# Two transformer blocks on one core: softmax weights divided before their transposes, two heads' values in one pass of column tiles, a new order of the first block's slots, and six gate units moved among the mixing units

## The reference

```python
def first_block(x, ...):            # 2 layers
    h = rms_norm(x, ln1_gain[l])
    proj = h @ w_in[l]              # q, k, v, gates and latents of three mixers
    o_nsa = nsa_mixer(...)          # 6 heads: gate0*compressed + gate1*selected + gate2*window
    o_mla = mla_mixer(...)          # 5 heads, softmax attention over 96 numbers
    o_ret = retention_mixer(...)    # 5 heads, decayed scores, group norm, silu gate
    mixed = concatenate([o_nsa, o_mla, o_ret])      # 384 + 320 + 320 columns
    x = x + mixed @ w_out[l]
    x = x + square(relu(rms_norm(x) @ w_up[l])) @ w_down[l]

def masked_softmax(s, mask):
    p = exp(s - max(s)) * mask
    return p / sum(p)

def hybrid_layer(x, ...):           # second block, 2 layers
    u = h @ w_in                    # pool, conv, q, k, v, gate_logits (3 x 1024)
    y_pool, y_conv = pool_mixer(...), b_conv * causal_short_conv(...)
    y_attn = moba_attention(q, k, v)                # 8 heads of 64
    merged = gates0 * (y_pool @ p_pool) + gates1 * (y_conv @ p_conv) + gates2 * (y_attn @ p_attn)
    x = x + g1 * (merged @ w_out)
    x = x + g2 * ((silu(h2 @ w_gate) * (h2 @ w_up)) @ w_down)
```

## Time and profile before

| | before |
|---|---|
| median of three runs | 1517.23 us (1515.48 to 1518.75) |
| the profiled execution, its own time | 1515.29 us |
| span of the profiled execution | 1513.5 us |
| busy share of the span: PE | 98% |
| PE weight load | 95% |
| DVE | 72% |
| ACT | 52% |
| POOL | 4% |
| granted clock of TensorE | 1.00 throughout |
| bytes moved | 296.56 MB, 195 GB/s over the span |

### The profile page before, as it was taken

The page is one execution under the profiler, slowest core; times in us unless marked ns, Lnnn a source line. Parts: engine busy times, 40 slices in busy tenths (PEclk is TensorE's granted clock), DMA queues, the critical chain, the costliest instruction groups (busy, mean ns, idle before and its releaser), DMA issues.

```text
span 1513.5 us, 29309 instructions
## 1 busy us (share of the span) xinstructions
PE 1481.1 (98%) x12148; PEld 1441.9 (95%) x12148; DVE 1085.0 (72%) x1931; ACT 783.4 (52%) x1370; POOL 63.3 (4%) x73
## 2 busy tenths in 40 slices
PE   8999999999999999999999999999999999999999
PEld 8888999999888999999999989999999999999999
DVE  8777788887777788788884577665569646766653
ACT  6555577435555487434555545444444554454442
POOL 0000000000000000000030030000003003100000
PEclk9999999999999999999999999999999999999999
DMA  8233389886234378887444444555434434454551
GB/s 327 80 142 121 142 308 341 325 335 259 101 113 167 140 265 328 325 341 271 165 161 149 168 143 151 197 179 195 173 144 158 168 141 167 139 194 170 194 184 67
DMA packets 42435, 296.56 MB, mean 196 GB/s; under 512 B 5056, under 2 KB 5312, under 8 KB 6848
## 3 DMA queue, kind: packets, MB, share of 16 engines
q1 hardware_dynamic: 41888, 294.67, 53.5%
q10 hardware_dynamic: 416, 0.02, 0.0%
HBM read 293.62 MB, written 1.05 MB: 195 GB/s over the span
## 4 chain that ended last, share of the span: by engine, by line
PE 74%; DVE 12%; DMA 6%; ACT 4%; issue 2%; POOL 1%; SPq 0%; DVEq 0%; ACTq 0%
PE acc L771 22%; PE acc L772 21%; PE acc L773 21%; DMA ring<-stream 6%; DVE wL L1688 5%; ACT wH L1333 2%; PE ps_t L898 1%; DVE ring L1678 1%; PE ps_s L885 1%; PE ps_o L908 1%; PE ps_o L907 1%; PE ps_s L883 1%; PE acc L972 1%; PE acc L867 1%; POOL region L2419 1%
## 5 line engine op out<-in xcount | busy, mean ns | idle before, releaser
L1688 DVE TENSOR_TENSOR wL<-ring,wH 128x1024 fp32r<-128x1024 f32 x444 | 548.5, 1242 | 276.8 <-ACT wH L1333 272.2
L771 PE MATMUL acc<-hH,wH 128*128 128x256 f32 x2240 | 648.0, 289 | 7.7 <-DVE wL L1688 3.2
L773 PE MATMUL acc<-hH,wL 128*128 128x256 f32 x2240 | 633.5, 283 | 0.0
L772 PE MATMUL acc<-hL,wH 128*128 128x256 f32 x2240 | 633.5, 283 | 0.0
L1333 ACT ACTIVATE wH<-ring 128x1024 fp32r<-128x1024 f32 x444 | 461.7, 1050 | 224.6 <-DMA ring<-stream 122.1
L771 PEld LDWEIGHTS acc<-hH,wH 128*128 128x128 f32 x2240 | 429.2, 192 | 14.0 <-issue 8.6
L772 PEld LDWEIGHTS acc<-hL,wH 128*128 128x128 f32 x2240 | 429.4, 192 | 3.5 <-issue 2.6
L773 PEld LDWEIGHTS acc<-hH,wL 128*128 128x128 f32 x2240 | 429.1, 192 | 0.0
L771 PE MATMUL acc<-aH,wH 128*128 128x256 f32 x864 | 245.4, 284 | 3.2 <-DVE wL L1688 3.2
L772 PE MATMUL acc<-aL,wH 128*128 128x256 f32 x864 | 244.5, 283 | 0.0
L773 PE MATMUL acc<-aH,wL 128*128 128x256 f32 x864 | 244.4, 283 | 0.0
(11 more groups left out here) (326 smaller groups left out, 1720.3 us busy)
## 6 DMA issues: line engine op xcount, KB each, us to landing
ring<-stream SPq DMA_DIRECT2D x276, 1024.0 KB, 4.9
cst<-consts SPq DMA_DIRECT2D x1, 1363.0 KB, 16.1
x<-xin SPq DMA_DIRECT2D x4, 256.0 KB, 3.7
out<-x SPq DMA_DIRECT2D x4, 256.0 KB, 4.2
onc<-once SPq DMA_DIRECT2D x1, 516.0 KB, 16.5
v1all<-vec SPq DMA_DIRECT2D x1, 355.0 KB, 8.9
v2all<-vec SPq DMA_DIRECT2D x1, 330.0 KB, 17.8
nv<-pos SPq DMA_DIRECT2D x1, 256.0 KB, 3.7
```

The costliest lines, as they stand in the source:

```text
L771: pe.matmul(out, w[0], y[0], start=first, stop=False)
L772: pe.matmul(out, w[0], y[1], start=False, stop=False)
L773: return pe.matmul(out, w[1], y[0], start=False, stop=last)
L1688: TTN(wL[:, n % SPLIT, :], ring[:, g % RING, half * UNIT:(half + 1) * UNIT], wH[:, n % SPLIT, :].bitcast(F32), ALU.subtract).then_inc(lo_r ...
```

## The change

1. **Weights are divided before their transposes.** In the first block `coefficients` (DVE) takes the reciprocal and the gate as before and multiplies the first 128 columns of a head's weights; `weights_normed` on ACT multiplies the other 256. PE's transposes of that head wait for both (`nf_ready`, `nw_ready`). The last `mla` head keeps the old way (`values_alone`, `output_alone`). In the second block DVE does both parts in two products.
2. **Values by pairs.** `group_values` and `paired_values` take v (64 columns) as the stationary operand and the transposed weights as the moving one, 256 and then 128 columns, with the two heads of a pair in the two halves of the array's columns. The output comes out transposed, so the transposes of chunks 0 to 4 (first block) and of `ya` (second block) are gone, as are DVE's products into `mixed` and `ya`. The `slc` and `win` branches of two heads add up in the same bank.
3. **Order of the first block.** `HEADS1` goes by r (slc r, slc 3+r, win r, win 3+r); the keys of the windows are projected before the slots, tiles of `tm` 1 before `tm` 0; feeds go one unit a slot; retention starts three slots earlier; the compressed outputs are made transposed; chunks 0 to 2 of `wout` run at slot 16, ahead of that slot's scores.
4. **Second block, mixing.** Of the 24 gate units six (numbers 6, 7, 14, 15, 22, 23) run between the mixing units, two after each pair of the first three; 18 stay in the attention. The sums go to `mgH`, `mgL` instead of `hH`, `hL`.

```diff
+MIX_TILES = [("mix", 0), ("gate", 3), ("mix", 1), ("gate", 7), ("mix", 2), ("gate", 11), ("mix", 3)]
+HEAD_GATES = [j for j in range(GATES // 2) if ("gate", j) not in MIX_TILES]
...
-HEADS1 = [(kind, h) for kind in ("slc", "win") for h in BY_QUERY] + [("mla", h) for h in range(MLA_HEADS)]
+HEADS1 = [(kind, h) for r in range(REP) for kind in ("slc", "win") for h in (r, REP + r)]
+HEADS1 += [("mla", h) for h in range(MLA_HEADS)]
...
 def fed_by(i):
...
+    return min(SIDE + SPLIT + 4 + i, 26)
...
+            def group_values(c, L):
...
+                pe.wait_ge(pt_copied, L * NH1 + (j + 3))
+                out = group_out
+                for part, (at, cols) in enumerate(((0, slice(0, S)), (2 * P, slice(P, S)))):
+                    for i in (j, j + 1):
+                        row = HD * (HEADS1[i][1] % 2)
+                        v = head1(i)[2][part]
+                        end = pe.matmul(out[row:row + HD, cols], v, prT[:, i % 2, at:at + cols.stop - cols.start],
+                                        start=first and part == 0, stop=last and part == 1)
...
                 for i in range(SLOTS1):
                     u = fill1(i)
-                    if u is None:
+                    if i == IN_PAIRS:
+                        chunk = side_by_side([f"wo{n}" for n in range(SIDE)], ms)
+                        for c in range(NSA_DONE):
+                            out_chunk(c)
...
+                    if i >= 3 and i % 2 == 1:
+                        group_values((i - 3) // 2, L)
...
+                    if 1 <= i <= IN_PAIRS:
+                        pe.wait_ge(nf_ready, L * IN_PAIRS + i)
+                        pe.wait_ge(nw_ready, L * IN_PAIRS + i)
                     if 1 <= i <= NH1:
                         weights_transposed(i - 1, NH1, 0, L)
-                    if i >= 2:
-                        values(head1, i - 2, NH1, 0, L)
...
+                def weights_normed(i):
+
+                    act.wait_ge(cf_ready, L * IN_PAIRS + (i + 1))
+                    w = pr[:, i % 2, P:3 * P]
+                    act.activation(w, w, ACT.Copy, scale=coef[:, i, 1:2]).then_inc(nw_ready, 1)
...
+                def coefficients(i):
+
                     kind, hh = HEADS1[i]
                     dve.wait_ge(p_ready, L * NH1 + (i + 1))
+                    done = nc.vector.reciprocal(coef[:, i, :], psumv[:, i, :])
...
+                    w = pr[:, i % 2, 0:P]
+                    TSC(w, w, coef[:, i, 0:1], None, ALU.mult).then_inc(nf_ready, 1)
...
-                for n in range(KC):
-
+                for kind, n in MIX_STEPS:
+
+                    if kind == "gate":
+                        project(f"g{n}", hs)
+                        continue
```

More of the change, by code:

```diff
@@ L57 @@
 TM_W = [256, 256, 256, TM1 - 768]
+MIX_TILES = [("mix", 0), ("gate", 3), ("mix", 1), ("gate", 7), ("mix", 2), ("gate", 11), ("mix", 3)]
+HEAD_GATES = [j for j in range(GATES // 2) if ("gate", j) not in MIX_TILES]
+HEAD_ORDER = [2 * j + half for j in HEAD_GATES for half in range(2)]
+MIX_STEPS = [(kind, 2 * j + half) for kind, j in MIX_TILES for half in range(2)]
 N_ADA, ADA_UP = 24, 10
@@ L96 @@
     + [(LATER2[2 * i], LATER2[2 * i + 1]) for i in range(4)]
-    + [("gate", j) for j in range(GATES // 2)]
-    + [("mix", j) for j in range(KC // 2)]
+    + [("gate", j) for j in HEAD_GATES]
+    + MIX_TILES
     + [("wout", j) for j in range(4)]
@@ L261, in order2 @@
     for i in range(NH2 + 2):
-        for n in gates_at(i):
-            out += [f"g{n}"] + ([f"yt{TURNED_AT[n]}"] if n in TURNED_AT else [])
-    for n in range(KC):
-        out += [f"{m}{n}" for m in MIXERS]
+        for k in gates_at(i):
+            out += [f"g{HEAD_ORDER[k]}"]
+    for kind, n in MIX_STEPS:
+        out += [f"g{n}"] if kind == "gate" else [f"{m}{n}" for m in MIXERS]
     out += [f"wo{n}" for n in range(KC)] + ["ss2"]
@@ L685, in late_bank, with nsa_chunk, halves @@
         def late_bank(c):
-            return {3: ps_s[0], 4: ps_s[1], 5: ps_s[0], 6: ps_s[1], 7: ps_t}[c]
+            return {5: ps_s[0], 6: ps_s[1], 7: ps_t}[c]
+        def nsa_chunk(c, rows=slice(0, P)):
+            return mixed[rows, :, P * c:P * c + P]
+        def halves(v):
+            return v.rearrange("p (t n) -> p t n", t=TT)
+        group_out = ps_o[:, 0:S]
         def product(n, m):
@@ new lines, in group_values @@
+            def group_values(c, L):
+                j = 2 * c
+                nsa = j < 2 * NSA_HEADS
+                g = c // 2 if nsa else REP + (c - NSA_HEADS)
+                first, last = (c % 2 == 0, c % 2 == 1) if nsa else (True, True)
+                if c == 0:
+                    drained("tm00")
+                    drained("tm01")
+                    if L > 0:
+                        pe.wait_ge(mla_out, L * 2)
+                elif 1 <= g <= REP and first:
+                    pe.wait_ge(nsa_out, L * REP + g)
+                elif g > REP:
+                    pe.wait_ge(mla_out, L * 2 + (g - REP))
+                pe.wait_ge(pt_copied, L * NH1 + (j + 3))
[6 more added lines that the diff above has]
+                                        start=first and part == 0, stop=last and part == 1)
+                if last:
+                    end.then_inc(group_full, 1)
@@ new lines, in paired_values @@
+            def paired_values(c, n, base, L):
+                j = 2 * c
+                pe.wait_ge(pt_copied, L * n + (base + j + 3))
+                if L > 0 or c > 0:
+                    pe.wait_ge(pair_drained, L * (n // 2) + c)
+                for part, (first, cols) in enumerate(((0, slice(0, S)), (2 * P, slice(P, S)))):
+                    for i in (j, j + 1):
+                        at = HD * (i % 2)
+                        v = head2(i)[2][part]
+                        last = pe.matmul(ps_o[at:at + HD, cols], v, prT[:, i % 2, first:first + cols.stop - cols.start],
+                                         start=part == 0, stop=part == 1)
+                last.then_inc(pair_full, 1)
@@ L1440, in taken @@
                         take_tokens(u)
[L1441 to L1444 removed]
+                        if u == "tm31":
                             act.wait_ge(acc_drained[A1.bank(u)], A1.drained(u, L))
@@ L2330, in _ @@
                                 .then_inc(acc_drained[A2.bank(f"{name}{n}")], 1)
-                        feed(44 + n + 1 + SPLIT)
-                    if n >= 2:
-                        dve.wait_ge(mgH_ready, L * KC + (n - 1))
-                        rest_of(hL[:, n - 2, :], merged[:, (n - 2) % 4, :], hH[:, n - 2, :]).then_inc(merged_ready, 1)
+                    feed(20 + len(HEAD_ORDER) + at + 1 + SPLIT)
+                    if kind == "mix" and n >= 2:
+                        merged_low(n - 2)
+                for n in range(KC - 2, KC):
+                    merged_low(n)
                 for n in range(KC):
```

384 lines of the change are left out of this document (201 added, 183 removed).

## The result

The changed kernel is slower: 1520.61 us median of 20 runs (1516.46 to 1534.71) against 1515.31 of the kernel before (20 runs beside it, 1511.76 to 1521.77). The ratio is 1.0040, 95% interval 1.0029 to 1.0052, so 6 us, 4.4 to 7.9. Forecast were 1508 us and a range of 1497 to 1518.

The account below looks back on a forecast made before the run. PE, busy 98% of the span, was taken as the bound. From the profiled 1515.3 us, -9.9 for the second block and +3.0 for the first gave 1508.4, forecast as 1508; the eight-in-ten range was 1497 to 1518.

Parts of the forecast that it names:

- Values by pairs: Both blocks' values on PE: a pair at 0.85 us instead of 1.24, saving 0.39 a pair.
- PE's work: PE's busy time over the whole kernel: down by some 12 us.
- Second block: Second block, less PE work and shorter mixing waits against new attention waits: -4.9 us a layer, -9.9 both.
- First block, waits in the slots: First block's slots: PE waits on the loop through ACT and DVE and on late work, 5.5 us a layer.
- Slot 16: First block, slot 16: PE waits for the third `wout` unit's feed, 3.0 us a layer, between 1.4 and 4.
- the step on the clock: First block: a clock under 1.00 anywhere there would be a cost not counted; nothing for it in the sum.
- the first block at full clock: First block's sum of saved work, new waits and waits that go: +1.5 us a layer, +3.0 both.
- the tail: First block behind the slots: of 2.28 us idle, 1.3 a layer goes with the wait for transposed chunks' low halves.
- Rival 1: First block: the loop fits everywhere, 3.9 us a layer gained, kernel at 1497.6 us; chance 0.20.
- Rival 2: First block: the loop is longer than PE's slot; at 6.4 us the kernel takes 1525; chance 0.11.
- Rival 3: Values: a pair's halves don't overlap, 1.24 us a pair saves nothing, 1517.8 us, at worst 1528; chance 0.13.
- Rival 4: Second block's mixing: last two units still wait for DVE and POOL, +3.3 us, 1511.7; inside the forecast's 0.56.

Follow-up runs that it names:

- e3: Changed kernel with 14 dummy products in slot 16's wait and the first two retention outputs a slot later: 0.9978 of the kernel before, 1513.37 us.
- e4: Kernel before with only the change's second block (division ahead, pairs, six gate units in mixing): 0.9946 of the kernel before, 1508.36 us.
- e9: e3 with no unit fed in slot 6 of the first block and two in slot 7: 0.9958 of the kernel before, 1509.04 us.
- e10: e9 with the weights of the first block's 16 heads neither divided nor gated: 0.9902 of the kernel before, 1500.94 us.
- e8: e4 with one DVE feed in the last mixing unit moved behind its product P: 0.9930 of the kernel before, 1504.23 us.
- e1: Changed kernel with 14 dummy PE products ahead of slot 16's first output chunk: 1.0023 of the kernel before, 1518.45 us.
- e2: Changed kernel with the first two retention outputs in slot 12 instead of 11: 1.0006 of the kernel before, 1518.23 us.

## Why the prediction was wrong

**Right.** *Values by pairs* at 0.85 us: 0.81. PE's work "down by some 12 us": the page shows only 6.2 less busy time (1481.1 to 1474.9), but time at half clock counts as busy there; in e3, without these falls, it is 1474.2 with 6.7 of dummy products in it (3.34 a layer), so 13.6 less. *Second block* -9.9: -9.1 by distances, -8.2 by e4's ratio; its mixing part was forecast at 40 to 42 us and takes 42.1 with one wait of 1.5, which I had at 0.5. *First block, waits in the slots*, 5.5 a layer: PE's idle time there is 6.0 in the first layer (71.00 - 65.55 and 21.70 - 21.13 in the stretches above) and 5.2 in the second. *Slot 16*, 3.0 out of bounds of 1.4 and 4: 3.6 (the lower bound is 1.7 by its own terms, 3.3 less 0.4, 0.85 and 0.32). ACT and DVE show why, in slot 15 of the changed kernel. First ACT, then DVE:

```profile
142.36 1.04 ACT L1381 ACTIVATE wH<-ring 128x1024 fp32r<-128x1024 f32 x1
143.30 0.36 ACT L1329 ACTIVATE region<-acc,rtok 128x146 f32<-128x146 f32 x1
143.70 0.74 ACT L1493 ACTIVATE region<-region 128x640 f32<-128x640 f32 x1
144.34 1.04 ACT L1381 ACTIVATE wH<-ring 128x1024 fp32r<-128x1024 f32 x1
```

```profile
143.43 1.23 DVE L1768 TENSOR_TENSOR wL<-ring,wH 128x1024 fp32r<-128x1024 f32 x1 [0.86 <-ACT wH L1381]
144.57 1.09 DVE L2163 TENSOR_TENSOR mtL<-region,mtH 128x256 fp32r<-128x256 f32 x3
...
146.13 1.23 DVE L1768 TENSOR_TENSOR wL<-ring,wH 128x1024 fp32r<-128x1024 f32 x1
```

PE is done with slot 15 at 143.9; the unit it needs is fed at 147.4, after evacuation, tanh, feed on ACT and two feeds, low halves and scores on DVE.

**Wrong: the step on the clock.** The prediction said of it that, if slot 16 let the clock fall, the sum would be "some us higher, inside the range", put nothing for it into the sum, and named a clock under 1.00 in the first block as a cost that it had not counted. It measured 5 us a layer, 10 in all (e3 against the change: 4.9 and 5.0 in the distances, 9.4 by the ratios), and made a gain into a loss. Two errors lie in that step. The price: the products behind slot 16's wait stood in the sum at their full-clock pitch, though the text held a wait of 3 us for likely and no row of the kernel before showed what follows such a wait. Half clock from 146 to 153 us is some 3.4 us a layer (an estimate: half of that time), 7 in all; had that been the only cost beyond the sum, the time would have been about 1515, inside the range, as the text said. And the place: only idle time was looked at, while the stretch from 118.8 us shows PE busy throughout and still at half clock, another 1.7 us a layer by the same estimate, behind a row of small products which the change had put together. The Trainium skill, "TensorE: Matmul & The Clock Gate", Part 1, says that an idle engine falls back to half its clock; slot 16 agrees (0.50 from 147.6 to 153.0 us), and the rule was cited but not priced.

**Wrong in size: the first block at full clock**, +1.5 a layer. With the clock held (e3) it is +3.4 and +3.3. Of the 1.9 us between, 0.6 is slot 16, and 0.9 the tail, which gave back 0.4 of the 1.3 credited: its idle time went from 2.28 us to 1.87 (13.00 - 11.13 in the stretches above). The rest has no place of its own in the rows. The feed that stands before an empty ring (e9, 0.7 a layer) the prediction didn't have at all; it lies within the idle time of the slots, whose sum came out right all the same, which is luck in part.

**The rivals.** None of the first three came. Rival 1 is refuted by the waits for divided weights, 3.7 us in the first layer. Rival 2, the loop too long for a slot, named the way the time moved, but not why: the loop does cost 4 to 5 us a layer (e10), and that was within the forecast, not beyond it. Its sum also leaves out the 3.0 us of slot 16, so it would have begun to be slower sooner than the text says. Rival 3 is refuted by 0.81 us a pair; the rule on draining at a change of tiling mode, which the prediction took from the Trainium skill, "TensorEngine Tiling (Array Packing)", Key Properties, shows no price in that row. Rival 4 came nearly as it was priced, half of 3.3 a layer, though for a feed of DVE more than for its last sums: 1.5 us of the 3.2 a layer stay ahead of the output tiles, until e8 took two thirds of them.

The balance, first layer of the first block: +4.9 clock (e3), +0.7 feed before the ring (e9), +5.2 division ahead of the transposes (e10), -2.5 for everything else (less work on PE, against the wait of slot 16): +8.3. The second block: -4.6 a layer.

## What to carry to other kernels

On a kernel that keeps PE at 98%, price a new wait twice: the idle time, and the products behind it at half clock, and look for rows of small products as well as for waits. A step put between exponentials and transposes makes a loop through three engines, and here it cost more than the waits that name it; where there are products with more slack around them (the second block) the same edit pays. When one change has parts in two places, measure them apart: the second block's part with its feed moved is 0.7% faster than the kernel before (0.9930, 0.9912 to 0.9947), and the whole change 0.4% slower.

## What the runs showed of the hardware

- A stretch in which PE was busy in every slice, but with products of 16 and 64 columns, was followed by 0.51 of the clock (118.8 to 122.3 us), in both layers, but in e1 in the second layer only; with those products spread out it wasn't there in any of seven kernels. What exactly decides it is open.
- Where the clock falls isn't fixed: with one place repaired it fell at others in some executions (432 us in e1 and e2; 29 us, ahead of the first scores, in nine of the fourteen profiled runs, behind a wait of 1.79 to 1.90 us; in two runs with a wait of 1.89 and 1.90 it didn't fall there, nor in the three with 1.46 to 1.54). The kernel before has a mean of 0.9998 over 31 runs and the changed one 0.9938 over 20, with no run above 0.996.
- The same code took different times in different executions where the weights stream fastest: from the last output product of the first block's second layer to the second block's first scores it was 258.8 to 267.7 us in the profiled runs, while the second block's attention was 62.64 to 62.67 in all eleven profiled runs that have the whole change there. A part of a kernel is better compared by such distances than by one execution's total.
